# Token columns of an input projection: 512 + 512 + 68 instead of 3 x 364

## What is computed

```python
def mixer_layer(h, ...):
    xn = rms_norm(h, norm_g)      # h: tokens x 2048
    z = xn @ w_in                 # w_in: 2048 x 11392, all projections in one
    ...                           # RWKV-7 recurrence, spatial gating
    m = jax.nn.sigmoid(gate_a) * ya + jax.nn.sigmoid(gate_b) * yb
    return h + m @ w_out, new_shift, S, vn
```

## Time and profile before

| | |
|---|---|
| median of 3 runs | 4152.35 us (4150.67 to 4154.87) |
| span of the profiled execution, first to last instruction | 4145.3 us |
| PE busy | 3927.6 us (95%), 26462 matmuls |
| PEld busy | 3802.6 us (92%), 26462 loads |
| DVE / ACT / POOL busy | 1452.6 / 459.1 / 421.4 us |
| granted TensorE clock, mean over the span | 0.974 |

### The profile page before, as it was taken

How to read it: one execution, slowest core, us unless ns; L and a number is a source line. 1 busy time by engine, 2 the same in 40 slices (tenths; PEclk the granted TensorE clock), 3 DMA queues, 4 the chain that set the end, 5 groups by cost and what they waited for, 6 DMA issues and landing times. The chain is left out here.

```text
span 4145.3 us, 59925 instructions
## 1 busy us (share of the span) xinstructions
PE 3927.6 (95%) x26462; PEld 3802.6 (92%) x26462; DVE 1452.6 (35%) x1723; ACT 459.1 (11%) x655; POOL 421.4 (10%) x300
## 2 busy tenths in 40 slices
PE   8999999999999999999996999999996699979994
PEld 7999999999999999999995888888885599979994
DVE  5121122112112112112116776777753733341123
ACT  2000000000000000000002333333322410020000
POOL 0000000000000000000003333333323200002110
PEclk9999999999999999999998999999997799999997
DMA  4112112112111111111102111111114433343225
GB/s 158 63 65 75 62 62 78 62 62 77 63 62 74 66 62 69 71 62 68 72 32 60 27 28 25 25 28 28 28 35 164 158 127 110 116 171 108 84 73 210
DMA packets 153965, 318.17 MB, mean 77 GB/s; under 512 B 98928, under 2 KB 99200, under 8 KB 140032
## 3 DMA queue, kind: packets, MB, share of 16 engines
q1 hardware_dynamic: 108816, 206.91, 15.2%
q10 hardware_dynamic: 44464, 108.51, 7.0%
q0 software_dynamic: 576, 1.08, 0.1%
HBM read 227.51 MB, written 88.96 MB: 76 GB/s over the span
## 5 line engine op out<-in xcount | busy, mean ns | idle before, releaser
L171 PE MATMUL in_acc<-in_xh,in_wh 128*128 128x364 f32 x4272 | 948.7, 330 | 1.7 <-issue 1.7
L171 PE MATMUL in_acc<-in_xl,in_wh 128*128 128x364 f32 x4272 | 941.7, 328 | 0.0
L171 PE MATMUL in_acc<-in_xh,in_wl 128*128 128x364 f32 x4272 | 941.5, 328 | 0.0
L171 PEld LDWEIGHTS in_acc<-in_xh,in_wh 128*128 128x128 f32 x4272 | 744.0, 188 | 6.0 <-issue 2.5
L171 PEld LDWEIGHTS in_acc<-in_xl,in_wh 128*128 128x128 f32 x4272 | 742.5, 188 | 0.0
L171 PEld LDWEIGHTS in_acc<-in_xh,in_wl 128*128 128x128 f32 x4272 | 740.7, 188 | 0.0
L310 DVE TENSOR_TENSOR in_stage<-in_acc,in_rstd 128x1092 f32<-128x1092 f32 x89 | 115.3, 1296 | 1689.2 <-PE in_acc L171 1689.1
L517 ACT ACT_TABLE_LOAD x17 | 21.8, 1283 | 2129.5 <-DVE mix L502 2129.2
L1132 POOL MEMSET gn_eps<- 128x1 f32 x1 | 0.1, 98 | 2182.6 <-POOLq L126 2182.6
L159 DVE TENSOR_TENSOR in_wl<-in_raw,in_wh 128x2048 fp32r<-128x2048 f32 x89 | 204.0, 2292 | 3.0
L171 PE MATMUL out_acc<-out_xh,out_wh 128*128 128x364 f32 x768 | 171.6, 332 | 22.0 <-DVE out_xl L1445 20.4
(11 more groups left out here) (220 smaller groups left out, 4160.3 us busy)
## 6 DMA issues: line engine op xcount, KB each, us to landing
in_raw<-in_w_in SPq DMA_DIRECT2D x89, 1024.0 KB, 4.8
z<-in_stage ACTq DMA_DIRECT2D x89, 548.0 KB, 2.7
mg_gate<-z SPq DMA_DIRECT2D x32, 546.0 KB, 3.6
mg_raw<-in_w_proj SPq DMA_DIRECT2D x32, 512.0 KB, 4.8
out_raw<-in_w_out SPq DMA_DIRECT2D x16, 1024.0 KB, 5.0
zin<-z SPq DMA_DIRECT2D x17, 812.5 KB, 5.5
mT<-mg_out ACTq DMA_DIRECT2D x16, 546.0 KB, 6.1
hT<-out_xs ACTq DMA_DIRECT2D x16, 546.0 KB, 3.4
```

Source lines behind the costliest of these rows:

```text
L171: mm = pe.matmul(self.acc[s][:, c, 0:NCH], w[s][:, k * P:(k + 1) * P], x[:, kx, c * NCH:(c + 1) * NCH], start=(k == 0 and w is self.wh and ...
```

## The change

`Gemm` takes a list of pieces: start and width of each. The input projection gives it `FULL`: 512, 512 and 68 columns. The merge and the output projection keep `EVEN`, three of 364. All that reads the input projection's accumulator follows: the sum of squares runs over the same pieces, the square root and the evacuation are two instructions each, one for the 2 x 512 columns (`wide`) and one for the 68 (`rest`). The evacuation's semaphore is raised by the second of them. Buffers keep their sizes (an accumulator has three banks of 512 in both).

```diff
@@ class Gemm
+    EVEN = ((0, NCH), (NCH, NCH), (2 * NCH, NCH))
+    FULL = ((0, 512), (512, 512), (1024, TP - 1024))
+
+    def __init__(self, nc, sc, tag, wt, kts, xh, xl, koff, parts=EVEN):
...
+        self.parts = parts
@@ Gemm.products
-                for c in range(3):
-                    mm = pe.matmul(self.acc[s][:, c, 0:NCH], w[s][:, k * P:(k + 1) * P],
-                                   x[:, kx, c * NCH:(c + 1) * NCH],
+                for c, (at, n) in enumerate(self.parts):
+                    mm = pe.matmul(self.acc[s][:, c, 0:n], w[s][:, k * P:(k + 1) * P],
+                                   x[:, kx, at:at + n],
@@ phase_in
-        gm = Gemm(nc, sc, "in", wt, KT, xh, xl, (0, 0))
+        gm = Gemm(nc, sc, "in", wt, KT, xh, xl, (0, 0), Gemm.FULL)
+        wide = lambda ap: ap[:, 0:1024].rearrange("p (c n) -> p c n", c=2)
+        rest = slice(1024, TP)
...
-                nc.scalar.activation(pieces(rstd[:, :]), gm.sums(1), ACT.Sqrt, bias=eps[:, 0:1]).then_inc(rt_ready, 1)
+                nc.scalar.activation(wide(rstd[:, :]), gm.acc[1][:, 0:2, :], ACT.Sqrt, bias=eps[:, 0:1])
+                nc.scalar.activation(rstd[:, rest], gm.acc[1][:, 2, 0:TP - 1024], ACT.Sqrt, bias=eps[:, 0:1]).then_inc(rt_ready, 1)
...
-                    dve.tensor_tensor(pieces(stage[s][:, ZO:ZW]), gm.sums(s), pieces(rstd[:, :]),
+                    dve.tensor_tensor(stage[s][:, ZO + 1024:ZW], gm.acc[s][:, 2, 0:TP - 1024], rstd[:, rest], MUL)
+                    dve.tensor_tensor(wide(stage[s][:, ZO:ZW]), gm.acc[s][:, 0:2, :], wide(rstd[:, :]),
                                       MUL).then_inc(gm.evacuated[s], 1)
...
-                    for c in range(3):
-                        mm = pe.matmul(gm.acc[1][:, c, 0:NCH], ones[:, :], sqb[n % 2][:, c * NCH:(c + 1) * NCH],
+                    for c, (at, width) in enumerate(gm.parts):
+                        mm = pe.matmul(gm.acc[1][:, c, 0:width], ones[:, :], sqb[n % 2][:, at:at + width],
```

More of the change, by code:

```diff
@@ L134 @@
 class Gemm:
-    def __init__(self, nc, sc, tag, wt, kts, xh, xl, koff):
+    EVEN = ((0, NCH), (NCH, NCH), (2 * NCH, NCH))
+    FULL = ((0, 512), (512, 512), (1024, TP - 1024))
+    def __init__(self, nc, sc, tag, wt, kts, xh, xl, koff, parts=EVEN):
         self.nc, self.wt, self.kts, self.xh, self.xl, self.koff = nc, wt, kts, xh, xl, koff
+        self.parts = parts
         self.raw = [sc.sb(f"{tag}_raw{s}", [P, kts * P]) for s in range(2)]
```

## The result

The changed kernel takes **4478.94 us** (median of 4 runs, 4476.68 to 4479.53) against 4153.61 us for the kernel before in the same comparison: ratio **1.0781**, 95% interval 1.0766 to 1.0796, or +325 us. The forecast was +337 us (4489 us).

The account below looks back on a forecast made before the run. PE's matmul stream in the input projection was taken as the bound: +78.6 ns a trio x 4272 = +335.8 us, +1.7 - 0.9 + 0.2 = +337 on 4145.3 us, plus 7 us to the median: 4489 us; range 4335 to 4520.

Parts of the forecast that it names:

- What bounds the stage: Input projection: one unbroken matmul stream on PE, 166.6 ns a matmul, 499.8 ns a trio (three pieces), 4272 trios.
- terms for group 0: First group: its trios' +78.6 ns each, sum of squares +1.7 us, PE idle time before group 1 -0.9 us.
- The rest costs a load, not its columns: 68-column piece: its columns take about 31 ns, but the longer load for the next 512 makes the step 111.8 ns.
- The price of 512 columns: Each 512-column F32R matmul: 233.3 ns if the surplus grows with columns, 228.2 if fixed, 215.8 if gone; 233.3 taken, 0.63.
- rival 1: 512-column matmuls: surplus doesn't grow (228.2 ns, 4446 us) or goes (215.8 ns, 4340 us); chances 0.15 (fixed or in between) and 0.11.
- the rule that was weighed there: Skill's warm matmul step, columns over 2.4 GHz plus 2.5 ns: 154.2 ns for 364 columns, 215.8 for 512.
- Rival 2: Weight load behind the rest doesn't bind, F32R weights loading in some 30 ns: trio 499.8 ns, 4153 us; chance 0.03.
- Rival 3: Next long piece's load pulled under the second 512, 512s without surplus: trio 462.4 ns, 3993 us; chance 0.04.
- sustained 131 ns: Skill's figure for pairs at 512 columns, weighed with rival 3: trio would fall far below 462.4 ns; given little weight.
- Rival 4: Narrow 68-column F32R piece split into two loads and two matmuls: another 111.8 ns, 4966 us; chance 0.04.
- The small terms: Outside the stream: sum of squares +1.7 us, idle between groups 0 and 1 -0.9, square root hidden, last evacuation +0.2.

## Why the prediction was right

- *What bounds the stage.* Right: the loss is 75.7 ns x 48 x 88 groups = 319.8 us, and 5.1 us by the start of group 1 (72.74 us instead of 67.60), and under 0.1 us at the end: 325.0 of the measured 324.9. The forecast's terms for group 0 (3.8 + 1.7 - 0.9) make 4.6 of the 5.1 us; group 1 starts anywhere from 67.1 to 68.2 us in the seven traces without an exposed load, which covers the rest. The granted clock stayed at 1.00 and DVE's idle time grew.
- *The rest costs a load, not its columns.* Right in mechanism: six runs with rests of 68 to 244 columns and one with half the weights follow it, and no rival does. The size was a little high: **108.5 ns** for the step (575.4 - 232.3 - 234.6), where 111.8 was taken from F32 matmuls of 128 columns. In the trace after, where two F32 matmuls of 68 columns end each sum of squares (59 ns from one to the next), the two loads behind them take 110 and 111 to 112 ns. So an exposed load beside F32 matmuls costs 2 to 3 ns more than one in the F32R stream; why, no run shows. With the sum of the two 512s a trio came out 3 ns below the forecast, x 4272 = 13 us: the whole difference between 337 and 325.
- *The price of 512 columns.* The choice between three values was the open part, and the one in proportion held: 232.3 and 234.6 ns, together 466.9 against the forecast's 466.6. So rival 1 (228.2 or 215.8) falls. No row behind the prediction had an F32R width but 364, so the choice was an argument, given 0.63; the widths of the last section bear it out. One of its reasons doesn't carry: the earlier trace rows was read as showing that the surplus isn't the load's, but the first two of those three matmuls step with loads under them, and the third gives a record and no step. With rival 1 falls for F32R the rule that was weighed there: by the step of the Trainium skill ("TensorE: Matmul & The Clock Gate", section "Back-to-back issue gap": columns over 2.4 GHz plus 2.5 ns) 512 would take 215.8 ns.
- *Rival 2* (a fast load for F32R): the load's step of 108 ns is seen in the open now, against 110 to 112 ns beside F32. The fast load of 128 weights that the Trainium skill ("TensorE: Matmul & The Clock Gate", section "Weight-path perf modes") describes for types other than FP32 isn't at work here.
- *Rival 3* (the load pulled under the second 512): no; the load behind a rest starts 2 to 4 ns after the rest became current, in all groups from the third on. The sustained 131 ns that was weighed with it stands in the Trainium skill's section "Back-to-back issue gap" of the same page; the 512s here took 231 to 235 ns. *Rival 4* (a split piece): no; 26462 records as before, and 194 ns in the mean for one of 68 columns.
- *The small terms.* Sum of squares and what lies between groups 0 and 1, PE and what it waits for, in the timeline after (L331 is L323, L163 is L159, L287 and L288 are L281 of before):

```profile
64.48 2.13 PE L331 MATMUL in_acc<-in_stage,in_ones 128*128 128x512 f32 x6
...
68.15 2.13 PE L331 MATMUL in_acc<-in_stage,in_ones 128*128 128x512 f32 x6
...
70.31 1.12 ACT L287 ACTIVATE in_rstd<-in_acc,in_eps 128x1024 f32<-128x1024 f32 x1 [4.84 <-PE in_acc L331]
70.38 2.29 DVE L163 TENSOR_TENSOR in_wl<-in_raw,in_wh 128x2048 fp32r<-128x2048 f32 x1
...
71.33 0.31 ACT L288 ACTIVATE in_rstd<-in_acc,in_eps 128x68 f32<-128x68 f32 x1
...
72.74 0.54 PEld L175 LDWEIGHTS in_acc<-in_xh,in_wh 128*128 128x128 f32 x3 [1.02 <-issue]
```

A k-tile of group 0 takes 3.67 us (64.48 to 68.15), 3.34 (six steps of 306 ns and nine of 166.6) + 0.34 = 3.68 were forecast. PE's pause ahead of group 1 shrank: the loads idle 1.02 us instead of the 1.94 in the earlier trace rows, -0.9 us as forecast. The second square root ends at 71.64, ahead of L163's end (72.67): hidden. The last evacuation runs from 2503.53 to 2504.90: 1.37 us instead of 1.29, so +0.08 us where 0.2 were allowed; the second instruction starts 0.08 us before the first has ended.

The 7 us between the profiled span and the runs' median, which the forecast adds, belong in the sum. But the reason given for them ahead of the prediction (what lies around the first and the last instruction) holds for 1.7 us of them: in every run with both on record, the time is 1.66 to 1.79 us above the span. The other 5 us are there because the execution that was profiled was a short one.

## What to carry to other kernels

In this stream a matmul that loads its own weights costs the longer of its columns and the load for the next one, so an uneven cut into full banks and a short rest is a loss where even pieces, or any pieces longer than a load, cost only their columns. Before cutting, read two numbers from the trace: the distance of two loads where a matmul waits for one (here 108 ns for 128 columns of 4-byte weights) and the step of a long matmul over its columns (here 0.45 ns); their quotient, some 240 columns, is the shortest piece that is free; the runs have 212 as not free and 244 as free. PE's busy share stays the same while this goes wrong; the loads' share and the number of matmuls in a fixed stretch show it.

## What the runs showed of the hardware that was not expected

- *The price of an F32R column hardly has a fixed part.* Mean distance from the moment a matmul starts to stream to the moment the next becomes PE's current one, by width: 68 columns 31.4 ns, 164 75.1, 212 97.7, 336 153.2, 364 166.6, 464 210.3, 512 232.3. From 68 to 512: 200.9/444 = 0.452 ns a column, and 0.6 ns left over at 68. At the granted clock of 2.4 GHz that is 1.086 cycles a column, where F32 has 2.00 between 364 and 512 columns ((429 - 305.5)/148 = 0.834 ns, the steps of the sum of squares after and before).
- *A column's price isn't quite the same everywhere.* In the kernel before, single steps of 364 columns lie between 160 and 184 ns, nine in ten of them between 161 and 171, and from the third group on the same place in each group has the same step to 1 ns. The same piece of 512 took 232.4 ns in one cut and 234.1 in another. With 64 columns of weights instead of 128, 364 columns took 165.3 instead of 166.6 ns. So the 8% above one column a cycle depend on something that recurs with the place in the loop; what it is, no run here settles. It stays open, and with it why 512 + 336 + 244 gained 2.5 ns a trio.
